# Moving the convolution's taps and product six steps later, with attention scores in other banks

## The reference, cut to what matters

```python
z = cg * xin                                   # branch C
z = depthwise_causal_conv(z, w_conv)           # three taps
out_c = bg * z                                 # the product
p = softmax(where(kpos <= qpos, q @ k.T * scale, -inf)); out = p @ v     # B and D, 8 heads in all
merged = sum(sigmoid(gate_i) * (branch_i @ w_branch[i]) for i in range(4))
x = x + rms_norm(merged @ w_out, g_post_mix)
```

## Time and profile before

| What | Value |
| --- | --- |
| Median of 3 runs | 792.83 us (792.43 to 793.06) |
| The profiled execution's own time | 792.57 us |
| Its span | 790.8 us |
| Busy: PE, DVE, ACT, POOL | 98%, 70%, 52%, 8% |
| Layer 0, from the first gate chunk to the end of the branch units | about 68.7 to 192.9 us |
| The same of layer 1 | about 457 to 581 us |

### The profile page before, as it was taken

One profiled execution on the slowest core, in us unless ns is written; L12 is line 12 of the kernel. 1 busy time (PEld: TensorE's weight loads), 2 busy tenths in 40 slices (PEclk: granted clock), 3 DMA queues, 4 the chain that ended last, 5 costly groups with the idle time before them and its releaser, 6 DMA issues.

```text
span 790.8 us, 11018 instructions
## 1 busy us (share of the span) xinstructions
PE 778.1 (98%) x3989; PEld 652.3 (82%) x3989; DVE 555.7 (70%) x826; ACT 411.4 (52%) x643; POOL 63.3 (8%) x86
## 2 busy tenths in 40 slices
PE   9999999999999999999999999999999999999997
PEld 6898788877888888888889987888678888888885
DVE  5689686789777566655666987766988856565663
ACT  7555755543475445444546656655336745444441
POOL 1210000006110000000020000000233000000000
PEclk9999999999999999999999999999999999999999
DMA  9686655544466656566826865655554675666631
GB/s 316 176 265 208 185 170 171 192 160 119 148 204 221 206 171 189 185 203 215 276 71 190 255 195 161 209 162 162 160 149 139 204 225 183 188 185 203 182 119 54
DMA packets 88201, 145.87 MB, mean 184 GB/s; under 512 B 10316, under 2 KB 51556, under 8 KB 88164
## 3 DMA queue, kind: packets, MB, share of 16 engines
q1 hardware_dynamic: 88020, 145.24, 58.8%
q10 hardware_dynamic: 144, 0.13, 0.1%
HBM read 144.31 MB, written 1.05 MB: 184 GB/s over the span
## 4 chain that ended last, share of the span: by engine, by line
PE 86%; DVE 8%; ACT 3%; DMA 1%; issue 1%; POOL 0%; POOLq 0%; DVEq 0%
PE banks L1406 21%; PE banks L1407 20%; PE banks L1408 20%; PE banks L1454 11%; PE banks L1455 5%; DVE w_lo L867 4%; PE banks L1458 2%; ACT w_hi L531 1%; DMA raw<-in_w_in_dram 1%; DVE probsT L989 1%; PE banks L1616 1%; DVE qkTB L1002 1%; PE banks L1457 1%; PE banks L1509 1%; PE banks L1418 1%
## 5 line engine op out<-in xcount | busy, mean ns | idle before, releaser
L867 DVE TENSOR_TENSOR w_lo<-raw,w_hi 128x1024 fp32r<-128x1024 f32 (+1 forms) x256 | 304.7, 1220 | 102.3 <-ACT w_hi L531 101.9
L531 ACT CAST w_hi<-raw 128x1024 fp32r<-128x1024 f32 (+1 forms) x256 | 257.6, 1043 | 119.1 <-PE banks L1458 45.8
L1406 PE MATMUL banks<-w_hi,xT_both 128*128 128x512 f32 (+2 forms) x472 | 182.0, 386 | 2.0 <-ACT gate_th L597 1.4
L1408 PE MATMUL banks<-w_hi,xT_both 128*128 128x512 f32 (+2 forms) x472 | 178.4, 378 | 0.0
L1407 PE MATMUL banks<-w_lo,xT_both 128*128 128x512 f32 (+2 forms) x472 | 178.4, 378 | 0.0
L1454 PE MATMUL banks<-xT_both,w_hi 128*128 128x512 f32 x364 | 130.4, 397 | 0.0
L1406 PE MATMUL banks<-w_hi,brT_hi 128*128 128x512 f32 x320 | 126.1, 394 | 3.4 <-DVE rows L1150 3.4
L1408 PE MATMUL banks<-w_hi,brT_lo 128*128 128x512 f32 x320 | 124.7, 390 | 0.0
L1407 PE MATMUL banks<-w_lo,brT_hi 128*128 128x512 f32 x320 | 124.6, 389 | 0.0
L1406 PEld LDWEIGHTS banks<-w_hi,xT_both 128*128 128x128 f32 x472 | 88.7, 188 | 23.1 <-ACT gate_th L597 3.1
L1408 PEld LDWEIGHTS banks<-w_hi,xT_both 128*128 128x128 f32 x472 | 88.7, 188 | 16.4
(11 more groups left out here) (197 smaller groups left out, 758.2 us busy)
## 6 DMA issues: line engine op xcount, KB each, us to landing
raw<-in_w_in_dram SPq DMA_DIRECT2D x88, 512.0 KB, 4.6
raw<-in_w_mlp_in_dram SPq DMA_DIRECT2D x64, 512.0 KB, 4.7
raw<-in_w_mlp_out_dram SPq DMA_DIRECT2D x64, 512.0 KB, 4.3
raw<-in_w_branch_dram SPq DMA_DIRECT2D x16, 512.0 KB, 4.0
raw<-in_w_out_dram SPq DMA_DIRECT2D x16, 512.0 KB, 4.1
gate_th<-in_w_in_dram SPq DMA_DIRECT2D x8, 512.0 KB, 8.6
raw<-in_w_in_dram SPq DMA_DIRECT2D x8, 352.0 KB, 5.8
x<-in_x_dram SPq DMA_DIRECT2D x4, 256.0 KB, 4.4
```

The source lines that it names most:

```text
L531: nc.scalar.copy(w_hi[:, c % RING, h * n:(h + 1) * n], raw_of(q)[:, 0:n]).then_inc(hi_ready, 1)
L867: v.tensor_tensor(w_lo[:, c % RING, cut], raw_of(q)[:, 0:n], w_hi[:, c % RING, cut].bitcast(F32), ALU.subtract).then_inc(lo_ready, 1)
L1406: nc.tensor.matmul(dst, l_hi, r_hi, start=first, stop=False)
L1408: return nc.tensor.matmul(dst, l_lo, r_hi, start=False, stop=last)
```

## The change

Scores go to banks 1 and 2 in place of 0 and 1; the last two pairs' values go to bank 0 in place of 2. In step 11 DVE does only the copy and the first product; the taps and the product with bank 0 stand in step 17, and the conversions of the result in step 20, behind those of branch A. The first pair's scores wait for `z_ready` in place of `c_out_ready`, and the third pair's values for `c_out_ready`. In the step after the scores ACT casts the first half of chunk s + 3 before the exponentials, and scales in the same step, behind the cast of the second half; DVE subtracts the first half behind the masks, takes the reciprocal, subtracts the second half and transposes five blocks. The other blocks come 5 and 6 in the next two steps. In step 28 DVE does three blocks, `gate_unit(0)`, three blocks, `gate_unit(1)`, and only then the split of chunk 31. No instruction is added or taken away.

```diff
--- before.py
+++ after.py
@@ -300,7 +300,7 @@
         BLOCKS = [(a, b) for a in range(4) for b in range(4)]
         FIRST_ORDER = [(g, t) for g in range(2) for t in range(T)]
         PROJ_ORDER = [(g, t) for t in range(T) for g in range(2)]
-        ORDER_C, ORDER_A, ORDER_B, ORDER_D = range(4)
+        ORDER_A, ORDER_C, ORDER_B, ORDER_D = range(4)
         LAST_PIECES = (slice(D // 2, 3 * D // 4), slice(3 * D // 4, D))
 
         UNITS = [(i, t, h) for i in range(2) for t in range(T) for h in range(2)]
@@ -682,13 +682,12 @@
                     act.wait_ge(ropeT_psum, nth(l, 2, 1))
                     nc.scalar.copy(kTD[D_NOPE:QK], psum[0:D_ROPE, 5, 0:S].unsqueeze(1).broadcast_to([D_ROPE, HEADS, S])
                                    ).then_inc(ropeT_copied, 1)
-                if s == 14:
+                if s == 20:
                     act.wait_ge(c_out_ready, nth(l, 1, 0))
                     branch_hi(l, 2, conv.rearrange("p f n -> p (f n)"))
                 if s - 1 in SCORES_AFTER:
+                    split_half(l, s + 3, 0)
                     pair_exp(l, SCORES_AFTER.index(s - 1))
-                if s - 2 in SCORES_AFTER:
-                    pair_normalise(l, SCORES_AFTER.index(s - 2))
                 if s == 19:
                     act.wait_ge(a_out_ready, nth(l, 1, 0))
                     branch_hi(l, 0, a_out)
@@ -750,13 +749,18 @@
                         split_half(l, s + 3, 1)
                     elif s == 10:
                         split(l, s + 3)
+                    elif s - 1 in SCORES_AFTER:
+
+                        side_step(l, s)
+                        split_half(l, s + 3, 1)
+                        pair_normalise(l, SCORES_AFTER.index(s - 1))
                     else:
                         side_step(l, s)
                         split(l, s + 3)
 
                 split(l, C_OUT)
                 act.wait_ge(attn_psum, nth(l, 4, 3))
-                branch_hi(l, 3, psum[:, 2, :])
+                branch_hi(l, 3, psum[:, 0, :])
                 split(l, C_OUT + 1)
                 split_half(l, C_OUT + 2, 0)
                 merged_hi(l, 0)
@@ -964,7 +968,7 @@
 
                 scale = -(float(HD) ** -0.5 if h < 4 else float(QK) ** -0.5)
                 dve.wait_ge(scores_psum, nth(l, 8, h))
-                bank = psum[:, h % 2, :]
+                bank = psum[:, 1 + h % 2, :]
                 apart(dve)
                 v.tensor_tensor_reduce(probs[:, h % 2, 0:P], bank[:, 0:P], causal[:, P:2 * P], scale, 3.0e38,
                                        ALU.add, ALU.min, neg_max[:, h % 2, 0:1]).then_inc(scores_masked, 1)
@@ -1074,6 +1078,7 @@
                     v.tensor_tensor(z[:, :, 2:S + 2], conv, banks[2], ALU.mult).then_inc(z_ready, 1)
                     dve.wait_ge(z_ready, nth(l, 2, 1))
                     dve.wait_ge(vec_copied, nth(l, 1, 0))
+                if s == 17:
                     for f in range(FT):
                         last = v.tensor_scalar(conv[:, f, :], z[:, f, 2:S + 2], vec_cols[:, 4 + f:5 + f], None,
                                                ALU.mult)
@@ -1086,7 +1091,8 @@
                                                           ALU.mult, ALU.add)
                         last.then_inc(conv_tap, 1)
                     dve.wait_ge(conv_tap, nth(l, 3, 2))
-                    v.tensor_tensor(conv, conv, banks[0], ALU.mult).then_inc(c_out_ready, 1)
+                    v.tensor_tensor(conv, conv, psum[:, 0, :].rearrange("p (f n) -> p f n", f=FT), ALU.mult
+                                    ).then_inc(c_out_ready, 1)
                 if s == 13:
 
                     dve.wait_ge(q_rope_copied, nth(l, 1, 0))
@@ -1119,10 +1125,8 @@
                         dve.wait_ge(probsT_ready, nth(l, 4, p - 1))
                     head_mask(l, 2 * p)
                     head_mask(l, 2 * p + 1)
-                if s - 2 in SCORES_AFTER:
-                    pair_inverse(l, SCORES_AFTER.index(s - 2))
-                if s - 4 in SCORES_AFTER:
-                    pair_transpose(l, SCORES_AFTER.index(s - 4), BLOCKS[10:])
+                    split_half(l, s + 3, 0)
+                    pair_inverse(l, p)
                 if s == 18:
                     dve.wait_ge(sv_psum, nth(l, 1, 0))
                     dve.wait_ge(u_gelu, nth(l, 1, 0))
@@ -1211,26 +1215,38 @@
 
                         side_step(l, s)
                         split_half(l, s + 3, 1)
+                    elif s - 1 in SCORES_AFTER:
+
+                        side_step(l, s)
+                        split_half(l, s + 3, 1)
+                        pair_transpose(l, SCORES_AFTER.index(s - 1), BLOCKS[:5])
                     elif s - 2 in SCORES_AFTER:
 
                         side_step(l, s)
                         split(l, s + 3)
-                        pair_transpose(l, SCORES_AFTER.index(s - 2), BLOCKS[:5])
+                        pair_transpose(l, SCORES_AFTER.index(s - 2), BLOCKS[5:10])
+                    elif s == C_BRANCH:
+
+                        side_step(l, s)
+                        pair_transpose(l, 3, BLOCKS[10:13])
+                        gate_unit(l, 0)
+                        pair_transpose(l, 3, BLOCKS[13:])
+                        gate_unit(l, 1)
+                        split(l, s + 3)
                     elif s - 3 in SCORES_AFTER:
 
+                        p = SCORES_AFTER.index(s - 3)
                         side_step(l, s)
-                        split(l, s + 3)
-                        pair_transpose(l, SCORES_AFTER.index(s - 3), BLOCKS[5:10])
+                        pair_transpose(l, p, BLOCKS[10:13])
+                        split_half(l, s + 3, 0)
+                        pair_transpose(l, p, BLOCKS[13:])
+                        split_half(l, s + 3, 1)
                     else:
                         side_step(l, s)
                         split(l, s + 3)
                     if 7 <= s < 11:
                         qk_transpose(l, BLOCKS[4 * (s - 7):4 * (s - 6)])
 
-                gate_unit(l, 0)
-                pair_transpose(l, 3, BLOCKS[10:13])
-                gate_unit(l, 1)
-                pair_transpose(l, 3, BLOCKS[13:])
                 gate_unit(l, 2)
                 gate_unit(l, 3)
                 split_half(l, C_OUT, 0)
@@ -1238,7 +1254,7 @@
                 split_half(l, C_OUT, 1)
                 for n in range(5, 8):
                     gate_unit(l, n)
-                branch_lo(l, 3, ORDER_D, psum[:, 2, :])
+                branch_lo(l, 3, ORDER_D, psum[:, 0, :])
                 split_half(l, C_OUT + 1, 0)
                 gate_unit(l, 8)
                 split_half(l, C_OUT + 1, 1)
@@ -1477,7 +1493,7 @@
 
                 if p == 0:
                     pe.wait_ge(qkTB_ready, nth(l, 1, 0))
-                    pe.wait_ge(c_out_ready, nth(l, 1, 0))
+                    pe.wait_ge(z_ready, nth(l, 2, 1))
                 if p == 2:
                     pe.wait_ge(ropeT_copied, nth(l, 2, 1))
                 if p >= 1:
@@ -1489,9 +1505,9 @@
                     heads.append((qTB[part, n // 2, :], kTB[part, n // 2, :]) if h < 4 else
                                  (qTD[0:QK, n, :], kTD[0:QK, n, :]))
                 for h, (q, k) in enumerate(heads):
-                    nc.tensor.matmul(psum[:, h, 0:P], q[:, 0:P], k[:, 0:P], start=True, stop=True)
+                    nc.tensor.matmul(psum[:, 1 + h, 0:P], q[:, 0:P], k[:, 0:P], start=True, stop=True)
                 for h, (q, k) in enumerate(heads):
-                    nc.tensor.matmul(psum[:, h, P:3 * P], q[:, P:S], k, start=True, stop=True
+                    nc.tensor.matmul(psum[:, 1 + h, P:3 * P], q[:, P:S], k, start=True, stop=True
                                      ).then_inc(scores_psum, 1)
 
             def pair_values(l, p):
@@ -1500,7 +1516,9 @@
                 if p == 0:
                     pe.wait_ge(u_gelu, nth(l, 1, 0))
                 f = p % 2
-                bank = psum[:, (3, 2)[p // 2], f * S:(f + 1) * S]
+                bank = psum[:, (3, 0)[p // 2], f * S:(f + 1) * S]
+                if p == 2:
+                    pe.wait_ge(c_out_ready, nth(l, 1, 0))
                 for t in range(T):
                     for h in range(2):
                         n = 2 * f + h
```

## The result

The changed kernel took 784.66 us (median of 5 runs, 783.96 to 784.97), beside 793.06 us for the kernel before on the same chip. The ratio is 0.9892, with a 95% interval of 0.9877 to 0.9906: 8.6 us of 792.83, between 7.5 and 9.8. The profiled execution took 784.97 us where that of before took 792.57, its span 783.2 where it was 790.8.

The account below looks back on a forecast made before the run. PE, busy 98%, was taken as the bound, its stalls worth at most 8.6 us. Terms 2 x 2.8 + 0.74 + 0.2 + 0.24 = 6.8 us off 792.57 gave 785.8, 786.0 for the median; range 784.6 to 788.6.

Parts of the forecast that it names:

- What bounds the kernel: Whole kernel: PE is busy 98%, so only its stalls can be won, some 8.6 us at most.
- Part 1, the stalls ahead of units 4 to 6: Steps 26 to 28: sooner scaling and weightings remove PE's three stalls, 2.4 us a layer.
- The walk: Step-by-step timing of the engines' queues on layer 0's old clock; for steps 26 onward it gave 2.8 us a layer.
- Part 1, "what is late next": POOL's additions, DVE's sums, third `w_out` chunk: a 0.3 us stall stays there; the stretch ends 2.8 us sooner a layer.
- The upper bound: Most for the stretch from the hand-over to the third `w_out` chunk: every stall there goes, 3.1 us a layer.
- The first rival: Additions and subtractions block each other, so the sums end later and the gain is 1.9 us a layer: 787.8; chance 0.15.
- Part 2, the convolution: Taps and product moved from step 11 to 17: chunk 14's stall shrinks, 0.74 us in layer 0, 0.2 in layer 1.
- The slack in the masks' chain behind step 17: Second pair's gate tanh ends at 107.9 where PE wants it at 109.1: slack 1.2 us.
- the cost if the cover goes: Step 17: without room from the earlier transpositions, the moved taps cost up to 3.1 - 1.2 us a layer.
- Part 3, chunk 16: ACT's copies stay ahead of the gate tanh, about 0.5 us of stall left; gain 0.12 a layer, 0.24 in all.
- The sum: Whole kernel: 2 x 2.8 + 0.74 + 0.2 + 0.24 = 6.8 us gained, 786.0 for the median; chance 0.63.
- The rival "all stalls go": Whole kernel: every listed PE stall goes, chunk 16's too, 8.6 us gained: 784.2; chance 0.05.

Follow-up runs that it names:

- number 3: Kernel before with only branch C's taps, product and conversions moved and banks changed, the old hand-over kept: 795.73 us, ratio 1.0042.
- experiment 8: Changed kernel with ACT's gate tanh of tile 1 put first in step 14 and ahead of the copies in step 16: 782.89 us, ratio 0.9873.
- experiments 1: Changed kernel with the split of chunk 31 first again in step 28, ahead of the last six transpositions and first two weightings: 787.04 us, ratio 0.9934.
- experiment 2: Kernel before with only DVE's step 28 in the new order, chunk 31's split last: 790.81 us, ratio 0.9972.
- experiment 5: Changed kernel with ACT's first half cast of chunk s + 3 behind the exponentials and gate tanh, together with the second: 784.82 us, ratio 0.9902.
- experiment 6: Changed kernel with POOL adding only 8 of 512 columns of branches 1 and 2: 784.61 us, ratio 0.9895.
- experiment 4: Changed kernel with branch C's taps, product and conversions back in steps 11 and 14: 785.16 us, ratio 0.9909.
- experiment 7: Changed kernel with ACT's gate tanh of tile 1 ahead of the four copies and the wide one in step 16: 783.67 us, ratio 0.9884.
- experiment 9: Changed kernel with both gate tanhs of tile 1 ahead in steps 14 and 16, branch C's taps, product and conversions back in steps 11 and 14: 782.58 us.

## Why the prediction was right or wrong, point by point

**What bounds the kernel: right, its ceiling too low.** The gain is PE's stalls, and nothing else moved: B and the stretch to chunk 26 agree to 0.01 us in all kernels but number 3. The stalls that the prediction lists add up to 2 x 2.81 + 0.79 + 0.24 + 2 x 0.73 = 8.1 us, not to the 8.6 that it names, and neither is the most that can be had: experiment 8 took 1.59 + 1.05 + 3.45 + 3.40 = 9.5 us off the same stretches.

**Part 1, the stalls ahead of units 4 to 6: right, and both halves of it needed** (experiments 1 and 2). The walk put weighting 0 at 168.1 and weighting 2 at 172.9; on the clock of before (the changed kernel is 0.38 us ahead at chunk 26 of layer 0) they came at 168.0 and 172.8. What the half cast ahead brings was overrated in its tone: 0.17 us a layer (experiment 5).

**Part 1, "what is late next": the step that failed, by its size.** The prediction kept a stall of 0.3 ahead of the third `w_out` chunk, gave 2.8 us a layer, and set 3.1 as the most. Measured were 3.45 and 3.40, which alone is 1.25 us more than forecast, where the whole difference is 1.0. The walk let additions and subtractions meet in an unlucky way: it took 11.1 us for the six additions (175.9 to 187.0), with the sums ending at 188.2. On the same clock they began at 175.9 as foretold and took 10.43, the sums ended at 187.5, and the split was ready 0.3 us before PE came. That POOL and DVE lengthen each other is shown (experiment 6), but the changed kernel has the slack to bear it. The upper bound was too low as well, though it let every stall go: the stretch U of layer 0 lost 2.56 us up to the first transposes of the sum, where the three stalls had been put at 2.39, then 0.72 up to the third `w_out` chunk, and 0.17 behind. The 0.33 us between 3.12 and 3.45 is matmuls that follow a stall or the transposes and start later than at a distance of 0.23, which the prediction counted behind some stalls only (behind unit 5's start at 175.16 the next is at 175.50, 0.34 us away). The first rival, which made this term smaller still, spoke in the wrong direction.

The port rule of the Trainium skill ("SBUF — State Buffer", "SBUF: two separate sides") names the pairs rightly: subtractions and sums lengthened, the weightings, with one input from PSUM, did not (0.67 to 0.69 beside additions or without). Its "fully blocks" fits 1.22 becoming 1.74, the rest of an addition and then the whole subtraction.

**Part 2, the convolution: the sign right, the sizes too high, and part of its reason missing.** Forecast 0.74 and 0.2 us in chunk 14; measured 0.54 and about 0 (layer 1 had 0.24 with the slower start behind the stall, and has 0.23). The walk had the scores in at 80.6, but the masks start 1.12 us after the first of them, which on that clock is 80.8; so the exponentials begin 1.46 us after the scores, where the walk had 1.3, and the tanh is 0.14 late. The prediction named `branch_lo` ahead of the masks and the sooner load of chunk 16 side by side; experiment 4 shows that the load decides. With the convolution unmoved, `branch_lo` is still there in both layers, and only the layer with the late load has more than the small stall. The layers' difference before, 0.79 against 0.24, which the prediction took for a property of the layers, was the time at which one load was issued, and in experiment 2 both layers had the large stall. So the 0.72 and 0.20 gained in A are what one execution of each kernel gave; against the trace of experiment 2 they would be 0.81 and 0.95. The slack in the masks' chain behind step 17 was there, 1.3 us where 1.2 was forecast (the tanh ends at 108.31, PE wants it at 109.65), and the cost if the cover goes, put at up to 3.1 - 1.2 = 1.9 us a layer, measured 2.0 (experiment 3).

**Part 3, chunk 16:** 0.12 a layer forecast, 0.19 measured. That the copies keep the stall was right, and that the order on ACT is the whole of it is shown (experiment 7).

**The sum.** 5.6 + 0.94 + 0.24 = 6.8 forecast; 6.85 + 0.54 + 0.38 = 7.8 measured on the trace. That parts 2 and 3 missed by 0.3 us only is luck in part, for chunk 14's share moves by 0.8 us with one load. The rival "all stalls go" gave 784.2; it came out near by time, but not by mechanism, since chunk 16's stall is still there.

## What to carry to other kernels

When an engine is 98% busy, list its stalls one by one from start to start, and ask of each what stands ahead of its releaser in that engine's own order; here the gate tanh moved ahead on ACT (experiment 9) did what a move of a whole stage was made for. A move that fills a gap has to be tested with the move that makes the gap, for alone it can cost (experiment 3). And the most that a stretch can give is better read as its whole length less the length of the same matmuls at their unstalled distance than as a sum of stalls: the sum left out 0.3 us a layer. Where one trace has two layers that differ, ask for a second trace before the difference is put into a forecast.

## What the runs showed that was not expected

- The load of chunk 16's second half lands at times that scatter by 0.9 us against the scores: where the convolution stands in step 11, its cast starts between 0.91 and 1.83 us ahead of them in the kernel before and in experiments 2 and 4, and PE's stall in chunk 14 follows. The load itself takes 4.6 to 4.9 us in all six cases; its issue moves. In three of the four late cases DVE had waited 0.91 us in step 7 for a result of POOL (`rstdD`), which it did in neither of the two timely ones; the fourth, layer 0 of experiment 2, is late without that wait, so what sets DVE's lead stays in part open.
- The start of the program scatters more than some of the effects: over the kernels of the study, whose programs are the same there, the transposes behind chunk 3 of layer 0 began between 31.7 and 32.9 us. A whole span can't tell 0.3 us. A stretch between two PE starts agrees much better where no load decides it: U to 0.02 us over the changed kernel and experiments 4 and 6 to 9, A to 0.1 over the changed kernel and experiments 1, 5 and 6.
